# The borders between stages: last products by output half, a shorter root, and another order of splits and weight slots

## What is computed

```python
h = x
for layer in range(2):
    f = swiglu(rms_norm(h, pre_g), w_gate, w_up, w_down)      # 1024 -> 2816 -> 1024
    h = h + 0.5 * rms_norm(f, post_g)
    m = gmlp_mixer(...) if layer == 0 else mla_mixer(...)      # ends in m @ w_out
    h = h + rms_norm(m, mix_post_g)
    f = swiglu(rms_norm(h, pre_g2), ...)
    h = h + 0.5 * rms_norm(f, post_g2)
# third layer: retention and forgetting attention, merged @ w_out, x = x + ..., swiglu, x = x + ff
# rms_norm(x, g) = x * rsqrt(mean(x*x) + 1e-6) * g
```

## Time and profile before

| what | value |
|---|---|
| median of 3 runs | 1486.06 us (1483.37 to 1489.32) |
| the profiled execution | 1487.02 us, span 1485.3 us |
| TensorE products busy | 1419.8 us (96%) |
| VectorE busy | 875.9 us (59%) |
| ScalarE busy | 768.7 us (52%) |
| GpSimd busy | 61.9 us (4%) |
| mean granted TensorE clock | 0.972 |
| HBM | 169 GB/s over the span |

### The profile page before, as it was taken

The page is one execution under the profiler, slowest core; times in us unless marked ns, Lnnn a source line. Parts: engine busy times, 40 slices in busy tenths (PEclk is TensorE's granted clock), DMA queues, the critical chain, the costliest instruction groups (busy, mean ns, idle before and its releaser), DMA issues.

```text
span 1485.3 us, 19638 instructions
## 1 busy us (share of the span) xinstructions
PE 1419.8 (96%) x6476; PEld 1163.2 (78%) x6476; DVE 875.9 (59%) x1328; ACT 768.7 (52%) x1233; POOL 61.9 (4%) x92
## 2 busy tenths in 40 slices
PE   7999999898999998999999899999998899999998
PEld 6888878677888877888877678888787767788887
DVE  6655565955655556555555675555644844665554
ACT  6555466435655546555554565554655523465552
POOL 0000010500000000000010000000100100000000
PEclk9999999999999999999999999999998866999999
DMA  8767536555666544766633456665546520465661
GB/s 271 228 198 221 174 122 205 155 172 162 211 199 205 185 141 142 221 196 191 184 112 102 135 172 195 196 192 144 153 137 181 179 78 29 155 214 184 193 188 57
DMA packets 199327, 251.65 MB, mean 169 GB/s; under 512 B 19718, under 2 KB 138084, under 8 KB 199276
## 3 DMA queue, kind: packets, MB, share of 16 engines
q1 hardware_dynamic: 199152, 250.97, 53.9%
q10 hardware_dynamic: 124, 0.03, 0.0%
HBM read 249.89 MB, written 1.05 MB: 169 GB/s over the span
## 4 chain that ended last, share of the span: by engine, by line
PE 88%; DVE 5%; ACT 3%; issue 1%; DMA 1%; SPq 1%; POOL 0%; DVEq 0%; ACTq 0%
PE ps L1643 27%; PE ps L1645 27%; PE ps L1644 26%; DVE wlo L1015 3%; PE ps L1669 2%; PE ps L1755 2%; ACT whi L554 1%; DMA raw<-in_w_in 1%; PE ps L2150 1%; PE ps L2152 1%; ACT sq_out L648 1%; ACT kthi L666 0%; PE ps L1887 0%; SPq L476 0%; PE ps L2049 0%
## 5 line engine op out<-in xcount | busy, mean ns | idle before, releaser
L1015 DVE SCALAR_TENSOR_TENSOR wlo<-raw,gcol,whi 128x512 fp32r<-128x512 f32 (+1 forms) x600 | 435.9, 774 | 295.9 <-ACT whi L554 294.6
L1643 PE MATMUL ps<-whi,kthi 128*128 128x512 f32 (+2 forms) x1400 | 556.8, 398 | 26.2 <-DVE wlo L1015 14.7
L1645 PE MATMUL ps<-whi,ktlo 128*128 128x512 f32 (+2 forms) x1400 | 546.6, 390 | 0.0
L1644 PE MATMUL ps<-wlo,kthi 128*128 128x512 f32 (+2 forms) x1400 | 546.2, 390 | 0.0
L554 ACT ACTIVATE whi<-raw,gcol 128x512 fp32r<-128x512 f32 (+1 forms) x600 | 397.2, 714 | 248.3 <-PE ps L1645 223.4
L1643 PEld LDWEIGHTS ps<-whi,kthi 128*128 128x128 f32 x1400 | 267.2, 191 | 83.0 <-issue 16.8
L1645 PEld LDWEIGHTS ps<-whi,ktlo 128*128 128x128 f32 x1400 | 266.9, 191 | 55.2
L1644 PEld LDWEIGHTS ps<-wlo,kthi 128*128 128x128 f32 x1400 | 267.6, 191 | 51.0
L1023 DVE TENSOR_TENSOR wlo<-raw,whi 128x1024 fp32r<-128x1024 f32 x151 | 182.7, 1217 | 129.3 <-ACT whi L558 128.7
L558 ACT CAST whi<-raw 128x1024 fp32r<-128x1024 f32 x151 | 156.2, 1046 | 157.9 <-PE ps L1645 146.8
L1643 PE MATMUL ps<-whi,hthi 128*128 128x512 f32 x440 | 172.1, 391 | 0.0
(11 more groups left out here) (192 smaller groups left out, 737.0 us busy)
## 6 DMA issues: line engine op xcount, KB each, us to landing
raw<-in_ffn_w_gate SPq DMA_DIRECT2D x176, 256.0 KB, 2.9
raw<-in_ffn_w_up SPq DMA_DIRECT2D x176, 256.0 KB, 3.1
raw<-in_ffn_w_down SPq DMA_DIRECT2D x176, 256.0 KB, 3.4
raw<-in_w_in SPq DMA_DIRECT2D x80, 256.0 KB, 3.4
raw<-in_gmlp_w_in SPq DMA_DIRECT2D x64, 256.0 KB, 3.1
raw<-in_w_gate SPq DMA_DIRECT2D x44, 256.0 KB, 2.9
raw<-in_w_up SPq DMA_DIRECT2D x44, 256.0 KB, 3.1
raw<-in_w_down SPq DMA_DIRECT2D x44, 256.0 KB, 3.3
```

The lines of the kernel that those rows point to most:

```text
L1015: ins = nc.vector.scalar_tensor_tensor(out=wlo[:, s, cut], in0=raw[:, s, cut], scalar=gcol[:, k:k + 1], in1=f32(whi[:, s, cut]), op0=ALU.m ...
L1643: nc.tensor.matmul(dst, lhs[0], rhs[0], start=first, stop=False)
L1644: nc.tensor.matmul(dst, lhs[0], rhs[1], start=False, stop=False)
L1645: return nc.tensor.matmul(dst, lhs[1], rhs[0], start=False, stop=last)
```

## The change

The last products of a stage are ordered by output half. In the last four chunks of `end_rows`, the last two run half 0 first, then half 1; in the last hidden tile of `ffn_rest` both chunks of half 0 come first, then both of half 1. A new semaphore `acc_half` tells of half 0, `tile0_done` or `slot_used` of half 1. ACT squares half 0 when `acc_half` says so, and DVE's gained half waits for the square of the same half (`acc_read` is gone). The mean goes into the square's scale, so the root's first two POOL steps become one. In `ffn_rest` two of four `then` stand before `gated_tile(1)` instead of three. In `after_rows` `then(2)` and `then(3)` come earlier, on both engines, and the last four chunks use slots 2, 3, 4, 5. In `opening`, tile 1 of h is turned ahead of slot 3 instead of slot 2.

```diff
-            root(f"post_{k}{t}", 1.0 / D / by ** 2, RMS_EPS / by ** 2, signals=2, halves=2)
+            root(f"post_{k}{t}", 1.0, RMS_EPS / by ** 2, signals=2, halves=2)
+            square_scale[f"post_{k}{t}"] = 1.0 / math.sqrt(D) / by
...
-        W_OUT = [0, 1, 2, 3, 4, 5] + [2, 3, 4, 5, 0, 1] + [4, 5, 2, 3]
+        W_OUT = [0, 1, 2, 3, 4, 5] + [2, 3, 4, 5, 0, 1] + [2, 3, 4, 5]
-        WO = [0, 1, 2, 3, 4, 5, 2, 3]
+        WO = [0, 1, 4, 5, 2, 3, 4, 5]
-        FOX_O = [2, 3, 4, 5]
-        OUT2 = [0, 1, 2, 3, 4, 5, 2, 3]
+        FOX_O = [4, 5, 2, 3]
+        OUT2 = [0, 1, 4, 5, 2, 3, 4, 5]
...
                 if halves == 2:
-                    step(nc.gpsimd.tensor_tensor(total, total, st("s_" + name)[:, 1:2], ALU.add))
-                step(nc.gpsimd.tensor_scalar(total, total, scale, eps, ALU.mult, ALU.add))
+                    step(nc.gpsimd.tensor_scalar(total, total, st("s_" + name)[:, 1:2], eps, ALU.add, ALU.add))
+                else:
+                    step(nc.gpsimd.tensor_scalar(total, total, scale, eps, ALU.mult, ALU.add))
...
@@ ffn_rest, ACT and (alike) DVE @@
                 if then:
-                    for s in range(3):
+                    for s in range(2):
                         then(s)
                 act.wait_ge(*last)
                 gated_tile(1, pre)
                 if then:
-                    then(3)
+                    for s in (2, 3):
+                        then(s)
                 turned_tile(1)
...
@@ after_ffn, ACT @@
+                acc_squares(post, 0, 0)
                 tile0()
-                acc_squares(post, 0, 0)
                 acc_squares(post, 0, 1)
-                act.wait_ge(*done)
                 acc_squares(post, 1, 0)
                 flip_high(0, 6)
+                act.wait_ge(*done)
                 acc_squares(post, 1, 1)
...
@@ after_ffn, DVE @@
-                tile0()
-                acc_gained(k, 0, 1)
-                dve.wait_ge(*sums(post + "0", 1))
-                acc_gained(k, 0, 0)
+                count("tile0_done")
+                acc_gained(post, k, 0, 0)
+                acc_gained(post, k, 0, 1)
                 renew(post, 0)
-                dve.wait_ge(*done)
-                acc_gained(k, 1, 1)
                 flip_low(0, 6)
-                dve.wait_ge(*sums(post + "1", 1))
-                acc_gained(k, 1, 0)
+                acc_gained(post, k, 1, 0)
                 flip_low(0, 7, 4)
+                acc_gained(post, k, 1, 1)
                 renew(post, 1)
...
@@ after_rows, ACT @@
+                    acc_squares(post, 0, 0)
                     tile0()
-                    acc_squares(post, 0, 0)
                     acc_squares(post, 0, 1)
+                then(2)
+                then(3)
                 flip_high(0, 6)
+                if post:
+                    acc_squares(post, 1, 0)
                 flip_high(0, 7, 4)
-                h_squares(pre, 0)
                 if post:
                     act.wait_ge(*done)
-                    acc_squares(post, 1, 0)
                     acc_squares(post, 1, 1)
-                then(2)
-                then(3)
+                h_squares(pre, 0)
                 flip_high(1, 6)
...
@@ after_rows, DVE @@
                 renewed(0)
+                then(2)
                 flip_low(0, 6)
+                then(3)
                 flip_low(0, 7, 4)
-                dve.wait_ge(*done)
                 if post:
-                    acc_gained(k, 1, 1)
-                    dve.wait_ge(*sums(post + "1", 1))
-                    acc_gained(k, 1, 0)
-                then(2)
+                    acc_gained(post, k, 1, 0)
+                    acc_gained(post, k, 1, 1)
+                else:
+                    dve.wait_ge(*done)
                 renewed(1)
-                then(3)
...
@@ opening, TensorE @@
-                        if t == 0 and s == 2:
+                        if t == 0 and s == 3:
                             flip_h(k, 1)
...
@@ ffn_rest, TensorE @@
-                down_chunk(0, 0, True)
+                down_half(0, 0, 0, True)
+                down_half(1, 0, 0, True).then_inc(sem("acc_half"), 1)
                 pe.wait_ge(sem("hid_ready"), b + 2 * NF)
                 hid_turn(7, 1, lambda c: c * P).then_inc(sem("hid_full"), 1)
-                down_chunk(1, 0, True).then_inc(sem("tile0_done"), 1)
+                down_half(0, 0, 1, True)
+                down_half(1, 0, 1, True).then_inc(sem("tile0_done"), 1)
                 pe.wait_ge(sem("ht_low"), b_ht + NF + 1)
-                for f in range(2):
-                    down_chunk(f, 1, True).then_inc(slot_used[4 + f], 1)
+                down_half(0, 1, 0, True)
+                down_half(1, 1, 0, True).then_inc(sem("acc_half"), 1)
+                down_half(0, 1, 1, True).then_inc(slot_used[4], 1)
+                down_half(1, 1, 1, True).then_inc(slot_used[5], 1)
```

More of the change, by code:

```diff
@@ L223, in build @@
         roots = []
+        square_scale = {}
         def root(name, scale, eps, n=1, signals=1, halves=1):
@@ L241, in after_rows @@
         def after_rows(k, following):
-            post(k, 0, 1.0); pre(following, 0); post(k, 1, 1.0); pre(following, 1)
+            post(k, 0, 1.0); post(k, 1, 1.0); pre(following, 0); pre(following, 1)
         pre("ffn00", 0); pre("ffn00", 1)
@@ L483, in _ @@
             all_rows(RET_O, chunked(a["w_ret_o_2"][0]))
-            all_rows(FOX_O, chunked(a["w_fox_o_2"][0]))
+            for c in (2, 3, 0, 1):
+                rows(FOX_O[c], take(FOX_O[c]), chunked(a["w_fox_o_2"][0]), c)
             sp.wait_ge(sem("rst_ready"), HR)
@@ L649, in squares @@
                                      else sq_out[:, t, part * BANK:(part + 1) * BANK], src, ACT.Square,
-                                     accum_out=st("s_" + name)[:, part or 0:(part or 0) + 1]).then_inc(sem("sum_ready"), 1)
+                                     scale=square_scale.get(name, 1.0), accum_out=st("s_" + name)[:, part or 0:(part or 0) + 1]).then_inc(sem("sum_ready"), 1)
             def acc_squares(name, t, half):
-                if half:
-                    act.wait_ge(sem("acc_read"), count("acc_read"))
+                if half == 0:
+                    act.wait_ge(sem("acc_half"), count("acc_half"))
                 squares(ps[:, 2 * t + half, :], f"{name}{t}", t, half)
@@ L965, in between_heads @@
                 if i == 4:
-                    highs(FOX_O[2:4])
+                    highs(FOX_O[0:2])
             exponentials("fox", 1.0, p2_sb, pt2_sb, lambda i, t: st("fox_sums", TT * H)[:, t * H + i:t * H + i + 1],
@@ L1585, in between_heads @@
                     fox_out(0)
-                    lows(FOX_O[2:4])
+                    lows(FOX_O[0:2])
                     yf_done[0] = latest(FOX_O[3])
@@ L1720, in opening, with row_half @@
                         ins.then_inc(sem("tile0_done"), 1)
+            def row_half(s, c, t, half, first, last):
+                rhs = slot(s, lambda x: x[:, half * BANK:(half + 1) * BANK])
+                return product(ps[:, 2 * t + half, :], kt(c, t), rhs, first, last)
             def row_chunk(s, c, t, first, last):
                 for half in range(2):
-                    rhs = slot(s, lambda x: x[:, half * BANK:(half + 1) * BANK])
-                    ins = product(ps[:, 2 * t + half, :], kt(c, t), rhs, first, last)
+                    ins = row_half(s, c, t, half, first, last)
                 return ins
@@ L1740, in end_rows @@
                 for t in range(TT):
-                    for c in tail:
+                    for c in tail[:2]:
                         if t == 0:
                             made(slots[c], take(slots[c]))
-                        if t == 1 and c == chunks - 1:
-                            flip_h(k, 0)
-                        ins = row_chunk(slots[c], c, t, c == 0, c == chunks - 1)
+                        ins = row_chunk(slots[c], c, t, c == 0, False)
                         if t:
                             ins.then_inc(slot_used[slots[c]], 1)
+                    for half in range(2):
+                        for c in tail[2:]:
+                            if t == 0 and half == 0:
+                                made(slots[c], take(slots[c]))
+                            if t == 1 and half == 0 and c == chunks - 1:
+                                flip_h(k, 0)
+                            ins = row_half(slots[c], c, t, half, False, c == chunks - 1)
+                            if t and half:
+                                ins.then_inc(slot_used[slots[c]], 1)
+                        if half == 0:
+                            ins.then_inc(sem("acc_half"), 1)
                     if t == 0:
@@ L1771, in hid_flip, with down_half @@
                     ins.then_inc(sem("hid_full"), 1)
+                def down_half(f, t, half, last, first=False):
+                    rhs = slot(4 + f, lambda x: x[:, half * BANK:(half + 1) * BANK])
```

(4 more changed lines are left out.)

22 lines of the change are left out of this document (9 added, 13 removed).

## The result

| | median us | executions | median, mean of the mean clock | us lost at half clock |
|---|---|---|---|---|
| before (beside the change) | 1484.36 | 20 | | |
| before (beside the first four runs below) | 1484.22 | 29 | 0.975, 0.9736 | 39.2 |
| after | 1490.63 | 20 | 0.970, 0.9698 | 45.0 |

The ratio is 1.0034, its 95% interval 1.0026 to 1.0043: **0.34% slower, 6.3 us**, where 5.2 us faster was forecast. The profiled execution after took 1489.82 us (span 1488.1, mean clock 0.969). One execution of the twenty took 7986.65 us; it is left out of the means and of the table of experiments.

A forecast was written before the change was run, and what follows sets the result against it. TensorE, busy 96% of the span, was taken as the bound, so only its waits and clock losses counted. Row borders -8.45, feed-forward borders +1.7 and clock +1.6 gave -5.2 us, 1480.9 us; range 1475.0 to 1487.5.

The forecast's parts named there:

- Row borders: Borders behind row products and the odd one: waits at turning tile 1 of h go; -4.3, -2.8, -1.35, together -8.45 us.
- No wait: Row border: TensorE turns tile 1 of h six products later, at 365.0, when h is already ready.
- some 0.2 in hand: Row border: six products (2.2 us) follow the turning, the low half takes about 2.0; a few tenths may show.
- Feed-forward borders: Four borders behind feed-forward stages: late htlo delays the next first product, +0.46 in three, +0.3 in the fourth; +1.7 us.
- 7 to 8: Sign in the list of waits: a new htlo wait of about 2 us, four times, 7 to 8 in all.
- The clock: One more fall of TensorE's clock to half among the feed-forward borders' still stretches, +1.6 us.
- each stretch is shorter than those after which it fell: Argument for few new falls: two still stretches of about 2 us stand where one of 2.8 stood per feed-forward border.
- The slower rival: htlo wait and turning drop the clock in every feed-forward border: eight falls, 12.8 us, giving 1492.1 us; chance 0.07.
- three or more: Sign that the forecast is wrong: the clock falls in three or more borders.
- The sum: Row borders -8.45, feed-forward borders +1.7, clock +1.6: -5.2 us, 1480.9 us after.
- The base: Median before taken from three runs, 1486.06 us, from which the forecast time was reckoned.
- Nothing put on: No time for the square's scale, slots of WO, FOX_O and OUT2, or earlier loads into slots 2 and 3.

The follow-up runs named there:

- the first four runs below: Changed kernel: three split pairs ahead 1481.73, tile 1 turned before slot 2 1487.78, late splits of slots 4, 5 1484.89; kernel before: two pairs ahead 1494.86 us.
- the first and the seventh section above: Changed kernel with three split pairs ahead of tile 1's gate, 1481.73 us; changed kernel with spare products in the waits on htlo, 1488.32 us.
- shifted versions: Kernel before with 6 or 14 needless products in the first mixer's opening, so everything behind comes later: 1486.98 and 1487.38 us.

## Why the prediction was wrong, step by step

- **Row borders, -8.45.** The waits at the turning went as said, and the two traces, product by product, show -4.4, -2.9 and -1.5 up to there. The step that failed comes behind "No wait": I followed the turning at `s == 3` to its low half ("some 0.2 in hand") and stopped. ACT's queue behind the copy sets when slot 0 is split for the second hidden tile, and the six products that I moved from behind the turning to ahead of it were what had covered it. Given back: 1.38 + 1.37 + 1.36 = 4.1 in waits, and a few tenths around them. The traces have -2.5, -1.4 and 0.0 in place of -4.3, -2.8 and -1.35: the term should have been -3.9.
- **Feed-forward borders, +1.7.** Right: from the first product on `hthi` to the next stage's first product, +0.41 and +0.40 in the first and fourth, against 0.46, and +0.02 in the second, against 0.3; in the third a fall lies between. The waits on `htlo` are 1.93, 0.81, 1.92, 1.93, 6.6 in all against "7 to 8".
- **The clock, +1.6.** The mechanism was named, its size was far off, and this term alone turns the sign. I counted two falls in six borders before and took one more, +1.6; with the fall of 1.76 us that the row term takes away, the forecast for the clock was -0.2 on balance. Measured on balance: 5.8 us more lost over all executions, so some 7.5 of new falls in place of 1.6. The argument "each stretch is shorter than those after which it fell" was worth nothing: 1.9 us brought a fall in 10 of 15, where 2.4 had in one of two. The slower rival had the sign ("from more than four falls on"), with fewer than its eight falls. It had the places only in part: the trace of after has one fall at the `htlo` waits and none at the turnings, and its sign of "three or more" borders was not met. The runs tie 3.4 to 3.6 of the 5.8 us to standing still at `htlo` (the first and the seventh section above); where the other 2 or so come from stays open.
- **The sum.** The fall that went from 367 us stands in the row term and also in the 5.8, so it must be counted once. Waits: -3.9 + 1.7 = -2.2 for the row borders, and +1.3 to +1.7 for the feed-forward borders, -0.5 to -0.9 together, against the measured -1.4 at full clock (give or take 0.7). With the clock's +5.8 the sum is +4.9 to +5.3, against +4.4 between the means (1490.1 and 1485.7; 1485.2 and so +4.9 beside the change) and +6.3 between the medians. So the miss of 9.6 us between the forecast's -5.2 and +4.4 is, within about 1 us, 6.0 of clock and 4.5 of row borders. The kernel before has most executions at one level (21 of 29 at 0.975 or above) and a few at 1488 to 1495, so its median lies 1.5 under its mean; after's executions spread evenly.
- **The base.** The 1486.06 of three runs was 1.7 above the 1484.4 of twenty; the range, 1487.5 at its top, was too narrow for a term that the rival set at 12.8.
- **Nothing put on** for the square's scale, slots and loads: no wait answers to them. The root's chain I priced at 1.0 us less in the row borders: h of tile 0 begins at 357.16 - 0.66 = 356.50 instead of 357.32, 0.8 less.

## What to carry to other kernels

When an instruction that another engine's queue waits for is moved later, follow that engine's whole queue behind it to the next thing TensorE needs, also into the next stage; the cover is the number of products behind the moved point. Ask of each wait not only how long it is but whether TensorE stands still in it: here a wait of 1.9 us with little work around it cost, on average over its places, 1.1 us more in clock, by one trace of each kernel. Where such a wait can't be removed, products that nobody needs, written to a free bank, kept the clock up in the windows behind them and won more than a tenth of a per cent, in both trials by little more than the noise.

## What was not expected of the hardware

- Falls of the clock come in steps of one size, 1.5 to 1.7 us of time each. The kernel before shows the same mean clock in many executions (0.975 in 18 of 29, 17 of 23 and 8 of 23), after in fewer (0.969 and 0.970 in 6 of 19 each).
- A wait of 1.3 us at 791 us brought a double fall (0.50 granted from 796 to 800) in every trace of a kernel with some part of the change, and none before the change or in its shifted versions, though that stretch is the same in all. Whether this is the order in the border ahead of it or the moment it is reached was not settled; filling the wait ended it.
- POOL's one step with two operands takes 0.30 us, the two it replaces 0.19 each, with 0.28 from one start to the next: 0.2 us saved, where I had counted the 0.28 of a step.
